# The third weight chunk of the attention's opening, prepared earlier on GpSimd, ScalarE and VectorE

## What is computed

```python
x = x + rms_norm(swiglu(rms_norm(x, g[2]), ffn_in, ffn_out), g[3])   # end of layer A
k, v = split(rms_norm(x, kv_norm_g) @ kv_w)                          # shared by all B layers
q = rms_norm(x, norm_g[1, 0]) @ q_w
# then attention over (128,1), (512,4), (2048,16) windows, with ALiBi
```

## Time and profile before

| | us |
|---|---|
| median of 3 runs | 2322.72 (2322.23 to 2322.91) |
| the profiled execution's own time | 2322.51 |
| its span (first to last recorded instruction) | 2320.7 |
| PE busy in the span | 2254.3 (97%) |
| DVE / ACT / POOL busy | 1509.0 / 940.1 / 477.8 |

### The profile page before, as it was taken

How to read it: one execution, slowest core, us unless ns; L and a number is a source line. 1 busy time by engine, 2 the same in 40 slices (tenths; PEclk the granted TensorE clock), 3 DMA queues, 4 the chain that set the end, 5 groups by cost and what they waited for, 6 DMA issues and landing times.

```text
span 2320.7 us, 32020 instructions
## 1 busy us (share of the span) xinstructions
PE 2254.3 (97%) x10792; PEld 1886.7 (81%) x10792; DVE 1509.0 (65%) x2236; ACT 940.1 (41%) x1712; POOL 477.8 (21%) x415
## 2 busy tenths in 40 slices
PE   7999997999999999999999999999799999999997
PEld 6888786888888888877888888888688888888886
DVE  5333347766666667697666666675876666666778
ACT  4111135322223234464655655565533323223443
POOL 1000014423332201053000000001543333310113
PEclk9999998999999999999999999999899999999999
DMA  5111122333333377736333323343233333337764
GB/s 146 46 55 45 51 94 64 96 99 108 104 108 106 108 263 249 252 108 173 75 69 77 77 69 73 73 114 114 73 95 104 110 105 109 101 111 260 249 224 168
DMA packets 244853, 273.98 MB, mean 118 GB/s; under 512 B 18400, under 2 KB 157664, under 8 KB 242656
## 3 DMA queue, kind: packets, MB, share of 16 engines
q1 hardware_dynamic: 241504, 260.64, 37.0%
q10 hardware_dynamic: 3200, 11.54, 1.5%
HBM read 198.20 MB, written 48.76 MB: 106 GB/s over the span
## 4 chain that ended last, share of the span: by engine, by line
PE 90%; DVE 4%; issue 2%; POOL 1%; ACT 1%; DMA 1%; DVEq 0%; SPq 0%; POOLq 0%; ACTq 0%
PE banks L1089 36%; PE banks L1136 15%; PE banks L883 11%; PE banks L1181 9%; PE banks L1012 7%; PE banks L1218 3%; PE banks L1233 3%; PE banks L1247 3%; PE banks L1261 1%; PE banks L931 1%; PE banks L1337 1%; DVE down_split L2212 1%; POOL xb_low L2731 1%; DMA raw_second<-in_o_w 0%; DVE x_lo L1933 0%
## 5 line engine op out<-in xcount | busy, mean ns | idle before, releaser
L1089 PE MATMUL banks<-xb_mid,up_split 128*128 128x512 f32 x2112 | 499.8, 392 | 4.7 <-DVE t_tile L1981 4.7
L1089 PEld LDWEIGHTS banks<-xb_mid,up_split 128*128 128x128 f32 x2112 | 400.5, 190 | 89.0 <-issue 5.5
L1136 PE MATMUL banks<-down_split 128*128 128x512 f32 x1848 | 423.0, 390 | 5.0 <-DVE down_split L2212 4.1
L1136 PEld LDWEIGHTS banks<-down_split 128*128 128x128 f32 x1848 | 345.6, 188 | 80.7 <-DVE down_split L2212 9.2
L1089 PE MATMUL banks<-xb_low,up_split 128*128 128x512 f32 x1584 | 373.5, 389 | 0.0
L1089 PEld LDWEIGHTS banks<-xb_low,up_split 128*128 128x128 f32 x1584 | 297.2, 188 | 62.2 <-issue 0.6
L2212 DVE TENSOR_TENSOR down_split<-down_raw,down_split 128x1024 fp32r<-128x1024 f32 x154 | 198.1, 1286 | 99.8 <-ACT down_split L1644 99.5
L1644 ACT CAST down_split<-down_raw 128x1024 fp32r<-128x1024 f32 x154 | 162.1, 1053 | 208.4 <-PE banks L1136 170.2
L2055 DVE TENSOR_TENSOR up_split<-sums,up_split 128x512 fp32r<-128x512 f32 x176 | 157.7, 897 | 130.0 <-ACT up_split L1499 129.7
L883 PE MATMUL banks<-x_hi,w_first 128*128 128x512 f32 x768 | 184.5, 392 | 1.2 <-ACT x_hi L1418 1.1
L2805 POOL TENSOR_TENSOR sums<-raw_up 128x512 f32<-128x512 f32 x88 | 119.6, 1361 | 320.3 <-DVE up_split L2055 162.2
(11 more groups left out here) (180 smaller groups left out, 3312.0 us busy)
## 6 DMA issues: line engine op xcount, KB each, us to landing
raw_up<-in_ffn_in_w SPq DMA_DIRECT2D x88, 512.0 KB, 5.1
down_raw<-in_ffn_out_w SPq DMA_DIRECT2D x154, 256.0 KB, 3.4
down_raw<-hid_spill SPq DMA_DIRECT2D x154, 256.0 KB, 4.0
hid_spill<-hid_mix SPq DMA_DIRECT2D x110, 256.0 KB, 2.4
down_second<-in_ffn_out_w SPq DMA_DIRECT2D x66, 256.0 KB, 3.2
k_stack<-k_parts SPq DMA_DIRECT2D x32, 512.0 KB, 6.2
raw_first<-in_conv_in_w SPq DMA_DIRECT2D x24, 512.0 KB, 3.7
hid_spill<-hid SPq DMA_DIRECT2D x44, 256.0 KB, 2.4
```

The lines of the kernel that those rows point to most:

```text
L1089: mm = pe.matmul(bank(b_out), up_split[:, p, a, q * P:(q + 1) * P], block(RIGHT_OF[p], b)[:, q, :], start=(i == 0), stop=(i == len(passes) ...
L1136: mm = pe.matmul(bank(b_out), side[:, a, 0, i * P:(i + 1) * P], side[:, b, 1, :], start=(p in (M3, M5, M1, M2) and first and j == 0), stop ...
```

## The change

Three instructions are moved, one on each of three engines; none is added or removed.

```diff
@@ ACT, down_layer
                 if pre:
+                    prepare(chunk0["attn"] + 2)
                     for t in range(HT + 1, TT - 1):
                         high_part(norm_ph, t)
@@ ACT, the attention's opening
             project((0, 0), 0, OPENING)
             high_part("norm2", TT - 1)
-            prepare(chunk0["attn"] + 2)
             project((0, 0), 1, OPENING)
@@ POOL, down_layer
                     if pre and q in (72, 73):
                         scale_chunk(q - 72)
+                if pre:
+                    scale_chunk(2)
                 for i in range(HT):
                     gain_left(i)
@@ POOL, the attention's opening
-            for c in (2, 3, 4):
+            for c in (3, 4):
                 scale_chunk(c)
```

## The result

| | before | changed |
|---|---|---|
| median, 16 runs each | 2321.67 us (2320.96 to 2322.91) | 2327.74 us (2326.85 to 2329.16) |
| ratio to before | | 1.0025, 95% interval 1.0018 to 1.0032 |
| profiled execution, its own time and span | 2322.51, 2320.7 | 2326.90, 2325.0 |
| PE, DVE, POOL busy | 2254.3, 1509.0, 477.8 | 2254.3, 1508.6, 476.1 |

The account below looks back on a forecast made before the run. From 1041 to 1060 us the norm's chain over DVE, ACT and POOL was the bound. 4.0 (wait on POOL) + 1.1 (low part) + 0.4 (clock) = 5.5 us on 2322.7 gave 2328.2 us, range 2325.2 to 2330.8.

Parts of the forecast that it names:

- Landing, scaling, left gains: POOL's queue ahead of the first root: landing 1035.3, scaling 1.90 us, four gains 7.1 us to 1044.3, root done 1045.3.
- The relief of DVE: DVE's splits no longer run beside left gains; the last products end 0.5 us earlier.
- Step 5: From DVE's first addition to `normed` of tile 4: 3.2 us late, 4.4 if POOL is caught; 4.0 us taken.
- the choice of the upper end: At `normed` of tile 4, 4.0 us taken between 3.2 and 4.4, because a POOL mean had taken 2.12 us.
- The moved low part and the first slow stretch: DVE's low part of chunk 2 ahead of tile 5's, +1.1 us; 1.2 GHz behind the wait before tile 4's turn, +0.4 us.
- The clock behind the key's start: PE behind the start of the key's second half: no added time forecast for the 1.2 GHz stretch there.
- Chunk 2 earlier buys nothing: PE wants chunk 2 only after 24 matmuls from 1060.40, over 6 us later; no gain from having it earlier.
- ACT at nothing: Chunk 2's high part moved ahead of tile 5's on ACT: 0, at most 0.5 us.
- given back later: Rival, 0.06: in the attention's first steps DVE's slack gives 1.8 of the 5.5 us back; 2326.4 us.

Follow-up runs that it names:

- pool_only: The kernel before with POOL's part of the change alone: chunk 2 scaled ahead of the left gains; +5.53 us, ratio 1.0023.
- landing_only: The kernel before, with the left gains waiting for the landing of chunk 2's DMA but its scaling left in place; +3.69 us, ratio 1.0013.
- low1_later: The kernel before, with chunk 1's low part on DVE moved behind `normed` of tile 4; -0.71 us, ratio 0.9994.
- splits_only: The kernel before with ACT's and DVE's part of the change alone, chunk 2 scaled behind the left gains; +1.36 us, ratio 1.0006.
- the filled kernels: The changed kernel, and the kernel before with POOL's part alone, each with unread matmuls in PE's two gaps; +3.90 and +4.63 us.
- after_filled: The changed kernel with 23 and 10 unread matmuls in PE's two gaps; +3.90 us, ratio 1.0021.
- before_filled: The kernel before with 9 unread matmuls ahead of the key's second half; -0.66 us, ratio 1.0000.
- gains_apart: The kernel before, with left gains 3 and 4 behind DVE's last split; -1.32 us, ratio 0.9996.
- best: The kernel before with left gains 3 and 4 and chunk 1's low part later, 9 unread matmuls and half the spill early; 2319.30 us, ratio 0.9990.

## Why the prediction was right

The direction and the mechanism were as forecast, and the sum, 5.5 us, lies at 5.8 by the ratio. Its terms did not all come out.

- **Landing, scaling, left gains.** Issued at 1030.69, landed 3.89 us later; scaling at 1034.65 (1035.3 forecast), 1.90 us long; the gains over at 1043.92 (1044.3), 7.3 us for four (7.1); first root done at 1044.81 (1045.3). These hold within 0.7 us. pool_only and landing_only show that this queue is the cause. The relief of DVE was undersized: the last products begin 1.17 us earlier by the common count, not 0.5.
- **Step 5, `normed` of tile 4.** Forecast +4.0, measured +3.07 in the profile, +3.3 by the common count. All of it is the delay of the first addition (1044.91 against 1041.84, 3.07 us, where 3.6 was forecast); from there to `normed` it is 5.26 us in both kernels. The step that failed is the choice of the upper end, "since that row is in just this sequence": no mean was caught for 2.12 us. POOL's catches there were a root of 1.45 us at 1045.15 and a mean of 0.86 us at 1046.60, one DVE instruction each (1044.91 and 1046.12), and the root of 1.47 us right ahead of `normed`, which the kernel before has too. The Trainium skill, "SBUF — State Buffer", section "Who interferes with whom", says that whoever issues first has the shared ports for the whole instruction while the other is fully blocked. Read as taking turns that gave 3.5 us, and these rows agree with it; low1_later agrees too. The row at 1042.19 with its two instructions in a row stays the exception, in every profile with that order.
- **The moved low part and the first slow stretch.** Forecast +1.1 and +0.4 on the way to the key's second half, measured +1.3 for the two (3.29 to 4.59). The low part's size is right (1.10 us in splits_only, 1.2 us between the filled kernels). The working covered part of the clock's cost with DVE's delay; in the changed kernel the two tie within 0.1 us at the turn of tile 7 (DVE's low part of tile 5 ends at 1061.02, PE's matmuls ahead of the turn at 1061.12), so that neither has a share of its own.
- **The clock behind the key's start.** Forecast at nothing, measured +1.5 (4.59 to 6.07). The second stretch was 6.8 us instead of 3.4: PE's 32 products from the key's start took 10.18 us instead of 9.00 (7.37 in after_filled), and the wait for `q_stack` is 0.3 us longer. This is the mis-sized term. The working had counted one more stretch, in a place with cover, and had not asked whether the one that was already there would be longer. Whether the change made it longer is not shown: splits_only has 6.8 us too behind the same 2.36 us of waiting that was followed by 3.4 us before.
- **Chunk 2 earlier buys nothing**: right. PE wanted it behind the 24 matmuls from 1064.77; DVE had it at 1059.88.
- **ACT at nothing**: right; pool_only, without ACT's move, has the same starts.

So at the key's second half 5.5 us were forecast (4.0 + 1.1 + 0.4) and 4.6 measured (3.3 + 1.3); behind it nothing was forecast and 1.5 us measured. That the sum was near is in part luck: 0.9 us too much in one place, 1.5 us too little in the other.

Of the rivals, "given back later" was nearest to something true. Little came back in the changed kernel, where PE waited 0.68 us for `q_stack` (0.38 before) and 1.16 us for DVE (1.39 before): +6.07 at the first scores is +5.83 at the second and +5.60 at 2280. But the wait for `q_stack` is what bounds before_filled, gains_apart and best, where PE comes to the scores earlier.

## What to carry over

On an engine that runs in order, ask of an instruction moved ahead what it waits for and when that lands, and add up everything queued behind it; idle time of that engine is no room if the wait ends after it. When a gap on TensorE grows, count each stretch at 1.2 GHz that may follow, the existing ones too, and lay it beside the other delays: those that run side by side do not add. Read what a change keeps behind the next waits too, and look for new waits far from the edit: a gain at the first scores was no measure of the gain at the second. A part freed at one place may come back as a collision further on, when a transfer lands earlier.

## What the runs showed of the hardware

- A wait of PE of 5.45 us and one of 2.54 us were each followed by 1.2 GHz, for 3.4 and 6.8 us; one of 3.42 us (landing_only) by none. The same wait of 2.4 us was followed by 3.4 us in the profile of before, 6.8 us in that of splits_only, and by none within the seam in gains_apart, where the clock fell only behind the wait of 2.24 us at the first scores. The 32 products behind that gap took 9.00, 10.23 and 7.39 us in these three. So the cost of one gap differs by up to 2.8 us between kernels that are alike at that place. Matmuls that no one reads kept it at 2.4 GHz in all five kernels that had them at the gap ahead of the key's second half.
- Three kernels with 33 added matmuls have a wait of PE of 2.04 to 2.14 us some 250 us further on, in the middle of a group, that the profile puts down to no engine or DMA.
- A DVE instruction on operands in on-chip memory (not PSUM) and a POOL instruction beside it: a subtraction of two such operands takes 2.25 instead of 1.21 us, an addition 2.90 instead of 1.23 us, a cast of one such operand 2.26 instead of 0.69 us (1064.63 in the changed kernel). The low parts `x_lo`, which read one operand from PSUM, never took more than 1.23 us.
- Copies from on-chip memory to on-chip memory kept the DMA engines full at 185 to 220 GB/s, where the stretches with the spill had 395 and 418 GB/s.
